# A decoder layer's lead-in: order of the products in a k step, and modulation sums formed for two k tiles at once

## What is computed

```python
c_act = jax.nn.silu(c)
shift, scale, gate = jnp.split(c_act @ w_ada[l] + b_ada[l], 3, axis=-1)
h = _rms_norm(x, norm_w[l]) * (1.0 + scale[:, None, :]) + shift[:, None, :]
proj = h @ w_in[l]
q, k, v, gate_a, u, gate_b = jnp.split(proj, splits, axis=-1)
...
y_a = _sliding_window_sink_attention(q, k, v, sinks[l]) * jax.nn.silu(gate_a)
y_b = _conformer_conv(u, conv_w[l], conv_b[l], ln_w[l], ln_b[l]) * jax.nn.silu(gate_b)
y = jnp.concatenate([y_a, y_b], axis=-1) @ w_out[l]
x = x + gate[:, None, :] * y
```

## Time and profile before

| | us |
|---|---|
| median of 3 runs | 431.35 (430.77 to 432.27) |
| the profiled execution, its own time | 431.71 |
| its span, first to last instruction | 430.0 |
| TensorE matmul busy | 408.4 |
| VectorE busy | 334.0 |
| ScalarE busy | 217.5 |
| GpSimd busy | 110.0 |
| mean granted TensorE clock, share of full speed | 0.996 |

### The profile page before, as it was taken

How to read it: one execution, slowest core, us unless ns; L and a number is a source line. 1 busy time by engine, 2 the same in 40 slices (tenths; PEclk the granted TensorE clock), 3 DMA queues, 4 the chain that set the end, 5 groups by cost and what they waited for, 6 DMA issues and landing times.

```text
span 430.0 us, 5914 instructions
## 1 busy us (share of the span) xinstructions
PE 408.4 (95%) x2102; PEld 327.6 (76%) x2102; DVE 334.0 (78%) x554; ACT 217.5 (51%) x496; POOL 110.0 (26%) x150
## 2 busy tenths in 40 slices
PE   0899998999999998999999999999999999999996
PEld 0577785888888887778776767777788888888886
DVE  2789777599999999999989797799995996222222
ACT  3768777025211137887788989524166784100000
POOL 1400050002420443354225316973031005100000
PEclk9999998999999999999999999999999999999999
DMA  7999656306930000004003466993637059951111
GB/s 274 353 316 351 243 178 207 99 0 167 231 61 2 6 8 7 7 2 155 0 8 91 75 124 124 166 103 71 125 74 124 2 195 252 259 125 49 50 49 50
DMA packets 54327, 51.40 MB, mean 120 GB/s; under 512 B 19271, under 2 KB 49275, under 8 KB 54298
## 3 DMA queue, kind: packets, MB, share of 16 engines
q1 hardware_dynamic: 38256, 41.50, 31.0%
q0 software_dynamic: 15904, 9.44, 16.8%
q10 hardware_dynamic: 138, 0.09, 0.1%
HBM read 46.82 MB, written 4.19 MB: 119 GB/s over the span
## 4 chain that ended last, share of the span: by engine, by line
PE 54%; DVE 28%; issue 3%; ACT 2%; DMA 1%; POOL 1%; DVEq 0%; ACTq 0%
PE pm L573 7%; PE pm L574 6%; PE pm L575 6%; DVE cacc L1326 4%; PE pm L846 4%; PE pm L845 4%; PE pm L847 4%; DVE cacc L1346 3%; DVE z L1333 3%; PE tr L846 3%; PE tr L845 3%; PE tr L847 3%; PE ps L702 2%; DVE cacc L1333 2%; DVE z L1346 2%
## 5 line engine op out<-in xcount | busy, mean ns | idle before, releaser
L573 PE MATMUL pm<-h,wts 128*128 128x512 f32 x224 | 90.4, 404 | 1.3 <-DVE gb L1461 0.8
L574 PE MATMUL pm<-h,wts 128*128 128x512 f32 x224 | 87.6, 391 | 0.0
L575 PE MATMUL pm<-h,wts 128*128 128x512 f32 x224 | 87.4, 390 | 0.0
L573 PEld LDWEIGHTS pm<-h,wts 128*128 128x128 f32 x224 | 42.2, 188 | 13.4 <-issue 2.4
L575 PEld LDWEIGHTS pm<-h,wts 128*128 128x128 f32 x224 | 42.2, 188 | 9.1
L574 PEld LDWEIGHTS pm<-h,wts 128*128 128x128 f32 x224 | 42.3, 189 | 8.2 <-issue 0.2
L921 ACT ACTIVATE wts<-raw 128x1024 fp32r<-128x1024 f32 x30 | 31.2, 1051 | 33.4 <-PE pm L575 17.4
L777 PE MATMUL pm<-wts,h 128*128 128x256 f32 (+1 forms) x128 | 45.1, 352 | 0.1
L778 PE MATMUL pm<-wts,h 128*128 128x256 f32 (+1 forms) x128 | 43.1, 337 | 0.0
L779 PE MATMUL pm<-wts,h 128*128 128x256 f32 (+1 forms) x128 | 43.1, 337 | 0.0
L440 POOL DMA_DIRECT2D wts<-in_w_in x22 | 28.8, 2697 | 51.6 <-ACT wts L923 51.6
(11 more groups left out here) (209 smaller groups left out, 901.7 us busy)
## 6 DMA issues: line engine op xcount, KB each, us to landing
slab<-in_w_ada SPq DMA_DIRECT2D x16, 512.0 KB, 8.2
raw<-in_w_in SPq DMA_DIRECT2D x14, 512.0 KB, 4.9
xs<-in_x SPq DMA_DIRECT2D x8, 512.0 KB, 8.8
raw<-in_w_ada SPq DMA_DIRECT2D x8, 512.0 KB, 4.5
xr<-in_x SPq DMA_DIRECT2D x8, 512.0 KB, 5.9
out<-xr SPq DMA_DIRECT2D x15, 256.0 KB, 2.7
wts<-in_w_in POOLq DMA_DIRECT2D x6, 512.0 KB, 9.5
raw<-in_w_in SPq DMA_DIRECT2D x8, 256.0 KB, 8.0
```

Of the source, the lines that this page charges most:

```text
L573: pe.matmul(out, hi_w, hi_x, start=first, stop=False)
L574: pe.matmul(out, lo_w, hi_x, start=False, stop=False)
L575: return pe.matmul(out, hi_w, lo_x, start=False, stop=last)
```

## The change

In each step the products with rounded h now run first (eight matmuls: hi and lo weights by hi h for all four banks), behind a wait for a new semaphore a_hr, which ScalarE raises once the rounded h of the tile is written; it now writes this before the float32 one. The four matmuls with the remainder follow, behind the wait for d_hlo. The columns of tile k + 1 move from ahead of the step to between its second and third bank, for all of k = 1 to 6. The filler of step 2 goes, with its wait; the filler before step 0 stands all ahead of the transposes and is half a 512-column matmul shorter there, and none follows them.

For tiles 4 to 7 the sums are formed for two tiles at once in `pair_acc` (128x512 operations on the whole slab pair): ScalarE's products behind modulate(2) and modulate(4), VectorE's first three sums behind split_h(2) and split_h(4), the other three and the final add behind split_h(3) and split_h(5), ahead of the weights' remainder. The buffers lie over `junk` and `ada_acc`, hence the waits for a_ssx and p_ada.

```diff
--- before.py
+++ after.py
@@ -79,6 +79,7 @@
     junk = at("junk", [D], F32, Z_AT + 6656)
     ada_acc = at("ada_acc", [2, 2, 2, P], F32, Z_AT + 10752)
     vrows2 = at("vrows2", [P], F32, Z_AT + 14848)
+    pair_acc = [at("pair_acc0", [2, 2, 2 * P], F32, Z_AT + 6656), at("pair_acc1", [2, 2, 2 * P], F32, Z_AT + 10752)]
     gacc = at("gacc", [D], F32, Z_AT + 10752)
     raw = at("raw", [3, 1024], F32, RAW_AT)
 
@@ -178,7 +179,7 @@
         a_cols, a_ssx, a_h32, a_hi, a_tanh = sem("a_cols"), sem("a_ssx"), sem("a_h32"), sem("a_hi"), sem("a_tanh")
         a_v, a_pt, a_exp, a_qT, a_sel = sem("a_v"), sem("a_pt"), sem("a_exp"), sem("a_qT"), sem("a_sel")
         a_pn, a_att, a_yhi, a_gbc, a_sq, a_ty = sem("a_pn"), sem("a_att"), sem("a_yhi"), sem("a_gbc"), sem("a_sq"), sem("a_ty")
-        a_link, a_prod, a_mix = sem("a_link"), sem("a_prod"), sem("a_mix")
+        a_link, a_prod, a_mix, a_hr = sem("a_link"), sem("a_prod"), sem("a_mix"), sem("a_hr")
 
         g_add = [sem(f"g_add{i}") for i in range(18)]
         a_neg = sem("a_neg")
@@ -562,10 +563,13 @@
                     pe.wait_ge(a_ab, 2 * (k - 1))
                 if k == 4:
                     pe.wait_ge(a_cols, 4)
-                pe.wait_ge(d_ada, sums_done(k, 6))
+                pe.wait_ge(d_ada, sums_done(k if k < 4 else 2 + k // 2, 6))
                 for part in range(2):
-                    last = pe.matmul(ada_bank(k)[:, part:part + 1], ada_acc[:, k % 2, 0, part, :], ones[:, 0:1],
-                                     start=True, stop=True)
+                    if k < 4:
+                        sums = ada_acc[:, k % 2, 0, part, :]
+                    else:
+                        sums = pair_acc[k // 2 - 2][:, 0, part, k % 2 * P:(k % 2 + 1) * P]
+                    last = pe.matmul(ada_bank(k)[:, part:part + 1], sums, ones[:, 0:1], start=True, stop=True)
                 last.then_inc(p_ada, 1)
 
             def three(out, hi_w, lo_w, hi_x, lo_x, first, last):
@@ -583,28 +587,28 @@
             ada_cols(0)
             keep_busy(pm[:, 2, :], 2)
             ada_cols(1)
-            keep_busy(pm[:, 2, :], 2)
+            keep_busy(pm[:, 2, :], 1)
+            keep_busy(pm[:, 2, 0:256], 1)
             x_transposes(0)
             x_transposes(1)
-            keep_busy(pm[:, 2, :], 1)
-            keep_busy(pm[:, 2, 0:256], 1)
 
             early = [(pm[:, 0, :], 1, 0), (pm[:, 1, :], 1, P), (pm[:, 2, :], 0, 0), (ps[:, 0, :], 0, P)]
             for k in range(KT):
                 if 0 < k < KT - 1:
                     x_transposes(k + 1)
-                    if k == 2:
-                        pe.wait_ge(a_ab, 4)
-                        keep_busy(ps[:, 1, 256:512], 4)
-                    if k > 1:
-                        ada_cols(k + 1)
-                pe.wait_ge(d_hlo, k + 1)
+                pe.wait_ge(a_hr, k + 1)
                 if k % 2 == 0:
                     pe.wait_ge(d_wlo, k // 2 + 1)
                 for e, (bank, slot, col) in enumerate(early):
-                    if (k, e) == (1, 3):
-                        ada_cols(2)
-                    last = channel_step(bank, slot, col, 0, k)
+                    if e == 2 and 0 < k < KT - 1:
+                        ada_cols(k + 1)
+                    for part in range(2):
+                        pe.matmul(bank, wts[:, slot + 1, part, k, col:col + P], h[:, 0, k, 0:HALF],
+                                  start=(k == 0 and part == 0), stop=False)
+                pe.wait_ge(d_hlo, k + 1)
+                for bank, slot, col in early:
+                    last = pe.matmul(bank, wts[:, slot + 1, 0, k, col:col + P], h[:, 1, k, 0:HALF],
+                                     start=False, stop=(k == KT - 1))
                     if k == KT - 1:
                         last.then_inc(p_main, 1)
                 if k == 0:
@@ -942,6 +946,17 @@
                     act.activation(ada_acc[:, k % 2, ct, :, :], slab_of(k, ct), ACT.Copy,
                                    scale=cact[:, ct:ct + 1]).then_inc(a_prod, 1)
 
+            def pair_products(q):
+
+                act.wait_ge(s_slab[q % 2][0], slab_due(2 * q))
+                if q == 2:
+                    act.wait_ge(a_ssx, 4)
+                else:
+                    act.wait_ge(p_ada, 4)
+                for ct in range(2):
+                    act.activation(pair_acc[q - 2][:, ct, :, :], slabs[q % 2][:, ct, :, :], ACT.Copy,
+                                   scale=cact[:, ct:ct + 1]).then_inc(a_prod, 1)
+
             def modulate(idx):
 
                 k = idx % KT
@@ -952,10 +967,10 @@
                 if idx >= 2:
                     act.wait_ge(d_hlo, idx - 1)
                 half = idx // KT
-                for dst in (h32[:, idx % 2, :], h[:, 0, k, half * HALF:(half + 1) * HALF]):
-                    last = act.activation(dst, tr[:, idx % 2, :], ACT.Identity, scale=modA[:, k:k + 1],
-                                          bias=modB[:, k:k + 1])
-                last.then_inc(a_h32, 1)
+                act.activation(h[:, 0, k, half * HALF:(half + 1) * HALF], tr[:, idx % 2, :], ACT.Identity,
+                               scale=modA[:, k:k + 1], bias=modB[:, k:k + 1]).then_inc(a_hr, 1)
+                act.activation(h32[:, idx % 2, :], tr[:, idx % 2, :], ACT.Identity, scale=modA[:, k:k + 1],
+                               bias=modB[:, k:k + 1]).then_inc(a_h32, 1)
 
             ada_products(0)
             ada_products(1)
@@ -983,10 +998,11 @@
                     act.activation(cols[:, 40:52], pv[:, 192:204], ACT.Copy).then_inc(a_cols, 1)
                 if k in (3, 5):
                     w_hi((k + 1) // 2)
-                if k + 2 < KT:
-                    ada_products(k + 2)
+                if k in (2, 4):
+                    pair_products(k // 2 + 1)
             w_hi(4)
             w_hi(5)
+            act.wait_ge(p_ada, 6)
             for t in range(4, NT):
                 sum_x(t)
 
@@ -1239,6 +1255,23 @@
                     dve.tensor_tensor(ada_acc[:, k % 2, 0, :, :], ada_acc[:, k % 2, 0, :, :], ada_acc[:, k % 2, 1, :, :],
                                       ALU.add).then_inc(d_ada, 1)
 
+            def pair_sums(q, cts):
+
+                for ct in cts:
+                    acc = pair_acc[q - 2][:, ct % 2, :, :]
+                    if ct % 4 == 0 or ct == 2:
+                        dve.wait_ge(s_slab[q % 2][ct // 4], slab_due(2 * q))
+                    if ct < 4:
+                        dve.wait_ge(a_prod, 8 + 2 * (q - 2) + ct - 1)
+                    else:
+                        dve.wait_ge(d_ada, sums_done(2 + q, ct - 4))
+                    dve.scalar_tensor_tensor(out=acc, in0=slabs[q % 2][:, ct, :, :], scalar=cact[:, ct:ct + 1], in1=acc,
+                                             op0=ALU.mult, op1=ALU.add).then_inc(d_ada, 1)
+                if cts[-1] == KT - 1:
+                    dve.wait_ge(d_ada, sums_done(2 + q, 5))
+                    dve.tensor_tensor(pair_acc[q - 2][:, 0, :, :], pair_acc[q - 2][:, 0, :, :], pair_acc[q - 2][:, 1, :, :],
+                                      ALU.add).then_inc(d_ada, 1)
+
             def split_h(idx):
                 half, k = idx // KT, idx % KT
                 sl = slice(half * HALF, (half + 1) * HALF)
@@ -1265,10 +1298,11 @@
             ada_sums(3)
             for k in range(2, KT):
                 split_h(k)
+                if k in (2, 4):
+                    pair_sums(k // 2 + 1, range(2, 5))
                 if k in (3, 5):
+                    pair_sums((k + 1) // 2, range(5, KT))
                     weights_lo((k + 1) // 2)
-                if k + 2 < KT:
-                    ada_sums(k + 2)
             weights_lo(4)
             weights_lo(5)
             for t in range(4, NT):
```

## The result

The changed kernel takes 437.24 (median of 6 runs, 433.84 to 439.97) against 431.58 for the kernel before on the same chip (6 runs, 430.77 to 432.27). The ratio is 1.0122, 95% interval 1.0071 to 1.0174: **slower by 5.7**. The forecast was 435.2, within 432.6 to 437.6. The direction and the two waits came as forecast; the clock cost nearly three times what I had put in. The six runs spread over 6.1 where those of before spread over 1.5, and that is part of the answer.

What follows compares the result with a forecast made beforehand. TensorE is busy 95% of the span; the end of modulate(7), 50.18, is where the lead-in sets the end. Waits 2.8 + clock 1.1 = 3.9 on 431.71 gives 435.6, less 0.36: 435.2, range 432.6 to 437.6.

Steps and rivals of the forecast that it cites:

- Step 0 and step 1: Lead-in: step 0 starts at 20.6 instead of 22.50; tile 3's sums end at 30.15 instead of 30.59.
- The step in its new order: TensorE in the lead-in: 3.7 per step; step 3 starts at 33.0 or 33.1 against 35.76, 2.7 ahead.
- The joint sums: VectorE in the lead-in: TensorE waits 2.5 and 2.4 at tiles 4 and 6; modulate(7) ends at 53.0, 2.8 late.
- The clock: TensorE falls to half speed after one of the two lead-in waits, costing 1.1; bounds zero and 3.3.
- case C: Both lead-in waits with two clock falls, or a longer cold stretch at 66 to 73: 437.3, chance 0.12.
- From 50.18 to the end: Behind modulate(7): everything waits for its predecessor on the chain, so the delay of 2.8 runs through undiminished.
- The link I named in between: ScalarE's two weight copies behind modulate(7), at 50.18, through which the lead-in sets the end.
- B: Both lead-in waits, no fall of TensorE's clock: 434.1, chance 0.30.
- D: Joint sums ready in time, lead-in steps run through at 3.7, modulate(7) ends 2.4 early: 428.9, chance 0.10.
- E: No difference: modulate(7)'s lateness doesn't reach the end, or waits half as long are paid by early gain: 431.4, chance 0.08.

Runs made afterwards that it cites:

- the order alone: Changed kernel with the sums of tiles 4 to 7 formed tile by tile again: 430.82 against 431.38 for the kernel before, ratio 0.9979.
- the version with the waits filled: Changed kernel plus five unread matmuls of ones (128x256) ahead of the columns of tiles 4 and 6: 434.02, ratio 1.0053 to the kernel before.
- the last set: Late weight copies moved ahead of modulate(7), in two versions VectorE's remainders too: 428.36, 429.69 (new order), 429.32 (order of before), against 432.08 for the kernel before.
- joint sums alone: Changed kernel with the order of before on TensorE and ScalarE, filler included, joint sums kept: 436.67, ratio 1.0127 to the kernel before.

## Why the prediction was right or wrong

**Step 0 and step 1.** Step 0 was to start at 20.6; it started at 21.05, and tile 3's sums were to end at 30.15 and ended at 30.54. This execution is 0.4 later from its first columns on (12.37 against 11.94 before), so the step is right.

**The step in its new order.** Step 3 at 33.0, measured 33.40, with the same 0.4. Right. (The undisturbed step of 3.64 that I called k = 3 is that of k = 2, from its first product at 32.12 to that of step 3 at 35.76; the length is the same.) What the order is worth at the end on its own I had not forecast: the 1.9 at step 0 and the 1.89 of filler became 0.2% in the order alone, where VectorE's sums hold the columns of tiles 5 and 7 for 0.47 and 0.46.

**The joint sums.** Taken at 0.67 from start to start and 0.69 for the add, from the convolution's rows; three took 2.07 and the add 0.69. Both waits were forecast at their places, 2.5 and 2.4 against 2.34 and 2.33, and what they cost the lead-in, 2.8, stands nearly as measured where the clock is kept up: 434.02 is 2.6 over the 431.38 of its set. The 0.59 that the prediction takes from the Trainium skill's page "VectorE: DVE Perf Modes" (its section on the TRN2 errata) is not what these operations took: they are 0.746 long on average and about 0.67 apart, as in the rows of before. With the page's figure the sum would have been 2.1, further from the 2.6. ScalarE's joint products, 0.72 each, cost nothing, and moving the second pair showed that slab transfers don't bind.

**The clock. This is the term that was mis-sized.** I took one fall, 1.1, and called two falls case C with a chance of 0.12. Measured: 3.2, the difference between the changed kernel and the version with the waits filled. Two things were wrong in it. I took one fall for two waits that are alike; the profiled execution has one after each. (One alone does occur, in the joint sums with the order of before.) And I let part of a fall pass while TensorE waits, hence 1.1 between 0.5 and 1.65. Both began behind their wait, at 38.8 where the wait ended at 36.9 and at 49.0 where it ended at 48.4, so all 3.4 of each fell on work, and each cost 1.6 by the two traces. All runs of the changed kernel, with the mean granted clock of each execution:

| mean clock | times | cold stretches of 3.4 |
|---|---|---|
| 1.00 | 433.84, 434.41 | none |
| 0.992 | 436.95, 437.52 | two |
| 0.988 | 438.37 | three |
| 0.984 | 439.97 | four |

The third column is worked out: (1 - clock) of a span of 433 to 438, over half of 3.4. Against the 434.1 of the first row each fall costs 1.4 to 1.6. That is no constant: before, 0.996 and 1.00 both occur, and the medians of the two groups in the last set are 432.2 and 431.3, 0.9 apart. What I had left out as well is that the number of falls is not fixed: the same program has none in two runs of six and four in one. A forecast from one profile should have carried that as the middle of the range and not as its edge. That the median lies inside the range, 0.4 under its upper end, is partly luck: two of the six runs, 438.37 and 439.97, lie above it.

**From 50.18 to the end.** That the delay runs through undiminished is right (6.1 at the weight copies, 6.5 at the convolution, 6.66 at the end). The link I named in between was the wrong one, as shown above; it moved nothing in the sum. The lower end of the range, 432.6 for waits one microsecond shorter each, doesn't follow from its terms either (431.35 + 2.8 - 2.0 = 432.2), nor quite the 437.3 of case C (431.35 + 2.8 + 3.3 = 437.5).

**Rivals.** B, both waits without a fall, is what a third of the runs are (434.1 forecast, 433.84 and 434.41 measured) and what the filler makes of all of them. C, 437.3, is the median. D fell with the lengths of the joint sums; the version that brings the joint sums of tiles 6 and 7 much earlier, and has no wait at tile 6, still takes 431.63 and not 428.9, with 1.41 of wait left at tile 4. E fell, since the waits were as long as forecast and the lateness did reach the end.

## What to carry to other kernels

Joining small operations saves work on the engine that runs them and makes their first consumer wait for the last part of the joint result; where an engine runs strictly in order, look at what stands between the parts, because here that was an operation (the remainder of tile 3 or 5) that had itself to wait for the step before. An idle stretch of two microseconds on TensorE can cost more than its own length: here, in four of six executions, 1.4 to 1.6 of clock for each fall besides. Either remove it or fill it, and judge by several runs with the clock of each, not by one profile. When a chain passes engines that wait for one another, test each link by moving its work; the one named last before a wait need not be the one that holds it.

## What the runs showed of the hardware

- A fall of TensorE's clock to its 1.2 GHz level lasted 3.4 each time in these traces. In the lead-in of the changed kernel one cost 1.6 by the traces, and 1.4 to 1.6 by the times; one in the kernel before, where the profiled execution has it between 70 and 73, about 0.9 by the medians of the runs with and without.
- Falls came after pauses of 2.34 and 2.33 (changed kernel), after one of 2.42 but not after one of 2.35 in the same execution (joint sums alone), and after two pauses of 0.56 and 0.47 (before without its filler). Executions of one program differ: the mean clocks of the changed kernel stand for none to four falls. With pauses of 1.43 and 0.75 in the lead-in, and the later ones of 0.3 to 1.4 between 65 and 73, 11 of 12 runs had one or two falls by their mean clock; with the lead-in's filled to 0.19, the mean clock was 0.999 or above in all six runs, though pauses of up to 1.07 follow from 68 on.
- GpSimd's operations on a single column lasted up to 1.41 instead of 0.54 while VectorE subtracted two operands of 128x1024 in SBUF, and 0.75 instead of 0.19 beside VectorE's normalisation of 128x1024.
